# GpSimd makes the low parts of weight units 11, 13, ... 25 in a two-block transformer kernel

## What is computed

```python
mod = silu(c) @ w_ada + b_ada                  # six vectors of 1024: sh1, sc1, g1, sh2, sc2, g2
h = rmsnorm(x, norm_gains[0]) * (1 + sc1) + sh1
proj = h @ w_in                                # queries, keys, values of 16 heads of 64
out_a = attention, heads 0 to 7 (full causal, bias by distance)
out_b = attention, heads 8 to 15 (window of 128, grouped keys, a sink per head)
y = concatenate([out_a, out_b]) @ w_out
x = x + g1 * rmsnorm(y, norm_gains[1])
```

## Time and profile before

| | |
|---|---|
| median of 3 runs | 789.35 us (789.23 to 792.32) |
| the profiled execution's own time | 793.4 us |
| its span in the profile | 791.7 us |
| its mean granted TensorE clock | 0.976 of full speed |

### The profile page before, as it was taken

How to read it: one execution, slowest core, us unless ns; L and a number is a source line. 1 busy time by engine, 2 the same in 40 slices (tenths; PEclk the granted TensorE clock), 3 DMA queues, 4 the chain that set the end, 5 groups by cost and what they waited for, 6 DMA issues and landing times.

```text
span 791.7 us, 12079 instructions
## 1 busy us (share of the span) xinstructions
PE 739.5 (93%) x4062; PEld 622.0 (79%) x4062; DVE 518.5 (65%) x764; ACT 449.5 (57%) x724; POOL 44.3 (6%) x77
## 2 busy tenths in 40 slices
PE   0599999979999999997999999999897999999998
PEld 0498966679999887775989777777686888888886
DVE  6886697678777744348657465665656777677443
ACT  1644677566666443355555587654546777777331
POOL 3100100100000100014102000000000000000000
PEclk9899999969999999999999999999997999999999
DMA  8999985237877655443774554544444566666651
GB/s 319 362 352 319 261 275 161 80 112 218 246 221 250 225 190 184 159 126 102 225 190 130 185 168 135 167 119 135 157 131 132 168 190 176 203 174 201 201 198 55
DMA packets 137166, 150.50 MB, mean 190 GB/s; under 512 B 6163, under 2 KB 111782, under 8 KB 137128
## 3 DMA queue, kind: packets, MB, share of 16 engines
q1 hardware_dynamic: 135278, 145.28, 59.2%
q10 hardware_dynamic: 1852, 4.75, 1.7%
HBM read 148.57 MB, written 1.44 MB: 189 GB/s over the span
## 4 chain that ended last, share of the span: by engine, by line
PE 85%; DVE 6%; ACT 3%; DMA 3%; issue 2%; POOL 0%; SPq 0%; POOLq 0%; DVEq 0%; ACTq 0%
PE acc L1363 14%; PE acc L1365 13%; PE acc L1364 13%; PE acc L1355 11%; PE acc L1342 7%; PE acc L1343 7%; PE acc L1344 7%; PE acc L1356 5%; DMA raw<-in_w_ada 3%; PE aux L1331 2%; PE aux L1527 1%; DVE wl L960 1%; PE aux L1501 1%; PE aux L1496 1%; DVE ada_sum L1038 1%
## 5 line engine op out<-in xcount | busy, mean ns | idle before, releaser
L960 DVE TENSOR_TENSOR wl<-raw,wh 128x1024 fp32r<-128x1024 f32 x217 | 266.0, 1231 | 151.6 <-ACT wh L594 150.8
L594 ACT ACTIVATE wh<-raw 128x1024 fp32r<-128x1024 f32 x217 | 227.9, 1055 | 124.2 <-PE acc L1365 111.3
L1342 PE MATMUL acc<-xT,wh 128*128 128x256 f32 x440 | 127.0, 289 | 5.5 <-DVE xT L990 4.1
L1355 PE MATMUL acc<-xT,wh 128*128 128x512 f32 x352 | 127.1, 405 | 0.8 <-DVE xT L982 0.8
L1343 PE MATMUL acc<-xT,wh 128*128 128x256 f32 x440 | 126.2, 287 | 0.0
L1344 PE MATMUL acc<-xT,wl 128*128 128x256 f32 x440 | 126.2, 287 | 0.0
L1363 PE MATMUL acc<-wh,xT 128*128 128x512 f32 (+1 forms) x272 | 110.0, 404 | 4.7 <-DVE xT L982 2.4
L1365 PE MATMUL acc<-wh,xT 128*128 128x512 f32 (+1 forms) x272 | 105.5, 388 | 0.0
L1364 PE MATMUL acc<-wl,xT 128*128 128x512 f32 (+1 forms) x272 | 105.2, 387 | 0.0
L1356 PE MATMUL acc<-xT,wl 128*128 128x256 f32 x352 | 100.1, 284 | 0.0
L1342 PEld LDWEIGHTS acc<-xT,wh 128*128 128x128 f32 x440 | 86.3, 196 | 7.5 <-issue 5.9
(11 more groups left out here) (260 smaller groups left out, 889.8 us busy)
## 6 DMA issues: line engine op xcount, KB each, us to landing
raw<-in_w_in SPq DMA_DIRECT2D x66, 512.0 KB, 3.6
raw<-in_w SPq DMA_DIRECT2D x64, 512.0 KB, 3.8
raw<-in_w_ffn_in SPq DMA_DIRECT2D x44, 512.0 KB, 4.4
raw<-in_w_ada SPq DMA_DIRECT2D x27, 512.0 KB, 6.2
raw<-in_w_ffn_out SPq DMA_DIRECT2D x22, 512.0 KB, 3.3
raw_more<-in_w_ada SPq DMA_DIRECT2D x13, 512.0 KB, 6.7
raw<-in_w_out SPq DMA_DIRECT2D x13, 512.0 KB, 4.3
rows_tmp<-in_w_ada ACTq DMA_DIRECT2D x8, 512.0 KB
```

The lines of the kernel that those rows point to most:

```text
L594: A(wh[:, s, :], raw_unit, ACT.Copy).then_inc(rounded, 1)
L960: V.tensor_tensor(wl[:, s, :], raw_slot(r), wh[:, s, :].bitcast(f32), ALU.subtract).then_inc(split_ready, 1)
L1342: mm(bank[:, 0:ROWS], wh[:, s, w], hi, start=(kt == 0), stop=False)
L1355: mm(bank[:, :], wh[:, s, w], moving[:, kt, :], start=(kt == 0), stop=False, skip_group_check=True)
```

## The change

For eight units, 11, 13, ... 25, the subtraction is taken from DVE and given to POOL. POOL makes six of them (11 to 21) ahead of its gain product and two (23, 25) behind it, each as soon as ACT has rounded the unit. A new semaphore `low_by_pool` counts them; PE waits for it where it needs such a unit. `split_ready` is still raised by DVE alone: at the next even unit DVE waits for POOL's part and then adds 2.

```diff
+POOL_LOW = [11, 13, 15, 17, 19, 21, 23, 25]
...
+            def low_unit(u):
+
+                pool.wait_ge(rounded, u + 1)
+                s = slot_of(u)
+                nc.gpsimd.tensor_tensor(wl[:, s, :], raw_slot(raw_place(u)[0]), wh[:, s, :].bitcast(f32), ALU.subtract)\
+                    .then_inc(low_by_pool, 1)
+
+            for u in POOL_LOW[:6]:
+                low_unit(u)
             pool.wait_ge(ada_used, (C_G1 + 1) * KT)
             pool.wait_ge(gain_loaded, 16)
             sums = ada_sum[:, D * C_G1:D * (C_G1 + 1)]
             nc.gpsimd.tensor_tensor(sums, sums, G1[:, :], ALU.mult).then_inc(gain_scaled, 1)
+            for u in POOL_LOW[6:]:
+                low_unit(u)
...
-            def low_unit(wait, r, s):
+            def low_unit(wait, r, s, made=1):
 
                 dve.wait_ge(rounded, wait)
-                V.tensor_tensor(wl[:, s, :], raw_slot(r), wh[:, s, :].bitcast(f32), ALU.subtract).then_inc(split_ready, 1)
+                V.tensor_tensor(wl[:, s, :], raw_slot(r), wh[:, s, :].bitcast(f32), ALU.subtract).then_inc(split_ready, made)
 
             def low_static(u):
-                if u < U_END:
-                    low_unit(u + 1, raw_place(u)[0], slot_of(u))
+                if u < U_END and u not in POOL_LOW:
+                    made = 1
+                    if u - 1 in POOL_LOW:
+                        dve.wait_ge(low_by_pool, POOL_LOW.index(u - 1) + 1)
+                        made = 2
+                    low_unit(u + 1, raw_place(u)[0], slot_of(u), made)
...
+            def low_ready(u):
+
+                if u in POOL_LOW:
+                    pe.wait_ge(low_by_pool, POOL_LOW.index(u) + 1)
+                else:
+                    pe.wait_ge(split_ready, u + 1)
```

More of the change, by code:

```diff
@@ L307, in build_program @@
         aux = [ctx.enter_context(nc.psum_tensor(f"aux{i}", [P, 512], f32)) for i in range(4)]
+        low_by_pool = sem("low_by_pool")
         first_full = [sem(f"first_full{i}") for i in range(FIRST_RING)]
@@ L1331, in transpose @@
                 return mm(out, in_, ident[0:n, 0:n], start=True, stop=True, is_transpose=True)
+            def low_ready(u):
[3 more added lines that the diff above has]
+                    pe.wait_ge(split_ready, u + 1)
             def col_unit(u, wait, bank, moving, waits=None):
                 s = slot_of(u)
-                pe.wait_ge(split_ready, wait)
+                if wait is None:
+                    low_ready(u)
+                else:
+                    pe.wait_ge(split_ready, wait)
                 for kt in range(KT):
@@ L1369, in narrow_half @@
                 s = slot_of(u)
-                pe.wait_ge(split_ready, u + 1)
+                low_ready(u)
                 for j in range(2):
@@ L1466, in proj1_unit @@
                         pe.wait_ge(acc_free, k - 3 if k < 8 else (9, 9, 9, 9, 10)[k - 12])
-                    col_unit(k, k + 1, acc[k % 4], xT, (lambda kt: X_COUNT * X_PROJ1 + 4 * (kt // 2) + 4) if k == 0 else None)
+                    col_unit(k, None, acc[k % 4], xT, (lambda kt: X_COUNT * X_PROJ1 + 4 * (kt // 2) + 4) if k == 0 else None)
                 else:
                     pe.wait_ge(acc_free, 11)
-                    pe.wait_ge(split_ready, k + 1)
+                    low_ready(k)
                     for r in range(RT):
@@ L1611, in _ @@
                         pe.wait_ge(acc_free, F_UP1 + k - 5)
-                    col_unit(u, u + 1, acc[(2, 3, 0, 1)[k - 4]], xT)
+                    col_unit(u, None, acc[(2, 3, 0, 1)[k - 4]], xT)
                 elif k < 12:
```

## The result

| | before | changed |
|---|---|---|
| median | 790.45 us, 10 runs (789.01 to 792.87) | 798.42 us, 10 runs (793.73 to 802.32) |
| ratio, 95% interval | | 1.0097 [1.0081, 1.0114] |
| profiled execution, span | 793.4, 791.7 us | 797.16, 795.4 us |

Slower by 0.97%, about 7.7 us, where +3.8 us was forecast; the interval lies above the 0.5% line, and 798.42 us above the range of 790.3 to 797.2. (1.1 us of that distance is the kernel before: 789.35 us from three runs then, 790.45 from ten now. The change itself was forecast at half its size all the same.) The runs also scatter more, 8.6 us against 3.9.

A forecast was written before the change was run, and what follows sets the result against it. PE was taken to bound the kernel, with DVE almost full behind it. The terms 2.6 - 1.5 + 0.5 + 0.8 - 0.3 + 2.25 - 0.55 gave +3.8 us on 789.35, so 793.2 us, range 790.3 to 797.2.

The forecast's parts named there:

- (a): Loads up to w18: 1.05 MB more ahead of them makes w18 and with it head 2 2.6 us later.
- (b): Ada item a28 behind head 2: POOL's gain product no longer holds it there, -1.5 us.
- (c): Unit 19: DVE is spared 1.1 us, POOL subtracts after a31 and a32 waits 1.6 us; net +0.5 us.
- (d): Unit 20's subtraction alone releases w19's slot, so w21 lands late and head 8's reciprocal follows; +0.8 us.
- Rival 1: PE's clock falls to 1.2 GHz after a stop around 124.5 to 127 us; +5.5 to +7.2 us, chance 0.25 (with lateness piling up).
- (e): Unit 21: DVE is spared 1.1 us, a37 waits 0.8 us for POOL's subtraction; -0.3 us.
- (f): POOL's gain product, now behind a37, goes in before a38 and delays it; +2.25 us.
- (g): PE's `weigh` of head 8 waits for the delayed `split` but had slack to spare; -0.55 us.
- rival 4: The two-element copy ahead of scores of heads 8 to 15 also waits for POOL; +4.0 us, chance 0.45 shared with forecast.
- Rival 2: The collisions at 119 to 125 us fall elsewhere, so (f) is gone; +1.6 us, 790.9 us, chance 0.22.
- rival 3: Not slower: w18 lands less than 1.5 us later and (b) outweighs (a); 788.4 to 789.5 us, chance 0.08.

The follow-up runs named there:

- e11: The kernel before, with POOL's gain product moved behind the last score of head 15; 790.64 us, ratio 0.9989.
- e12: e1 with units 19 and 21 back on DVE and the gain product behind unit 17; 790.61 us, ratio 0.9994.
- e14b: e12 with the gain product moved behind the last score of head 15; 790.02 us, ratio 0.9993.
- e1: The changed kernel, but SP gets an odd unit's raw place back from POOL's own semaphore; 793.04 us, ratio 1.0032.
- e3: The changed kernel with POOL's gain product moved behind unit 23; 796.90 us, ratio 1.0077.
- e8: The changed kernel with the edits of e1 and e3 together; 791.43 us, ratio 1.0021.
- e6: The changed kernel with four extra PE products, results unused, in each of the steps of heads 4 and 5; 797.83 us, ratio 1.0087.
- e2: The changed kernel with DVE making all low parts, odd units' raw places still released one unit late; 794.55 us, ratio 1.0057.
- e9: e2 with only units 11, 13 and 15 released one unit late; 794.97 us, ratio 1.0041.
- e13b: The changed kernel with units 19 and 21 back on DVE and released on time, gain product moved ahead to unit 17; 794.79 us, ratio 1.0051.
- e10: e2 with only units 17 to 25 released one unit late, 11 to 15 by their own subtraction; 793.25 us, ratio 1.0023.
- e4: The kernel before, with POOL's gain product waiting until all 40 ada items are used; 791.67 us, ratio 1.0006.

## Why the prediction was wrong

The direction and most of the mechanisms held, and the chance given to slower (0.47) was nearly that given to "within 0.5%"; the size was half of what came.

**What bounds the kernel**: right. PE's 0.9 us of waits were all that could be won (the stages of e11, e12 and e14b are 0.7 us shorter), and DVE at 19.17 of 20 us had no reserve: e1, with two subtractions and the gain product between 100 and 121 us, loses 0.32%, and e12, with none of them there, nothing.

**(a), (b)**: right. 2.6 and 1.28 us were measured, and the stage was 1.1 us late at head 2. w16's rounding came at 80.2 in the stage's time (80.4 said), with 0.7 us of PE's waiting. That this is "taken back before 101 us" is only half so: PE waits 0.54 us at 102.93 for w18's sake, which hides it. In e3's profile w18 came 0.9 us earlier, PE doesn't wait there, and head 2 is still 0.6 us late after 1.3 at head 1.

**(c), +0.5: the step that failed.** It said that POOL begins unit 19 when a31 ends, and so meets a32. But POOL waits for nothing except the rounding, and unit 19 is rounded before a31's turn comes, so POOL goes in first and a31 itself is held. The rows of the kernel before say so already, and the prediction didn't use them: unit 19 was rounded from 100.79 to 101.84, and a31 followed at 102.11.

```profile
100.79 1.05 ACT L594 ACTIVATE wh<-raw 128x1024 fp32r<-128x1024 f32 x1
```

```profile
102.11 1.28 DVE L1038 SCALAR_TENSOR_TENSOR ada_sum<-raw,cT,ada_sum 128x1024 f32<-128x1024 f32 x1
```

A subtraction of 2.39 us from 101.9 on ends at 104.3, and a31 1.08 us behind it, at 105.4 instead of 103.39: an estimate of 2.0 us of hold from the rows of before, where 2.2 was measured. It counts in full, because a31 stands ahead of head 4's reciprocal, and the subtraction that DVE was spared (1.1 us) behind it. All kernels with unit 19 on POOL bear this out. In us from the start of each span; the last column is the time from head 2's `weigh` to head 3's, less the 3.61 of before:

| kernel | unit 19 rounded | a31 recorded | POOL starts | held up | step at head 3 |
|---|---|---|---|---|---|
| changed | 103.96 | 103.99 | 104.03 | a31, 2.2 us | 2.2 us |
| e3 | 103.39 | 103.76 | 103.46 | a31, 1.9 us | 1.8 us |
| e1 | 100.37 | 101.33 | 100.45 | a31, 1.3 us | 1.25 us |
| e8 | 100.40 | 101.40 | 100.47 | a31, 1.2 us | 1.2 us |
| e6 | 104.51 | 104.40 | 104.59 | POOL, then a32, 1.0 us | 0.9 us |

Only in e6, where ACT had waited 0.26 us for w19, was unit 19 late enough for a31 to be first. That w19 is issued 10 us later in the stage's time (99.38, and 88.44 before) was not followed by the sum either, but it worked towards the assumed order, not against it.

**Rival 1, 0.25, happened**: PE's clock. I had put it at the stop of 124.5 us; it followed the 2.1 us stop of step (c), and cost 1.6 us more in this profile. (The 3.4 us stretch that rival 1 reckons with stands in none of its rows; the trace of before has one at 358 to 362 us.) It differs from profile to profile: those of e2 and e9 have 6.8 us of it, those of e3 and e13b, with stops of 1.7 and 1.8 us, none. That it makes the scatter of 8.6 us is likely and not shown: the mean granted clock of each execution was 0.972 in the slowest of the changed kernel (802.32 us), 0.980 in the fastest (793.73) and 0.976 to 0.979 between, and in e3 0.970 at 801.34 and 0.981 at 791.80. But this is a mean over the whole program, and e6 has 0.972 at 798.88 us, 1.9 us above its fastest.

**(d), +0.8: right in place, too small for the release alone.** w21 was issued at 114.92 (113 said, and 112.43 in e10, where nothing else is late), and landed some 5.3 us later where 4.3 was taken from the earlier trace rows. Without the late w18 (e10) it costs 1.5 us of the stage and 0.23% of the time. In the changed kernel most of it was hidden by lateness that was there already, the slow clock's among it: ACT waited only 0.61 us for w21.

**(e), (f), (g) with rival 4**: +2.25 - 0.3 - 0.55 forecast, and together with (d) +2.2; the stage lost 1.6 there. The copy of two elements did wait (rival 4, without which the gain product would have met a38 and not a37), and PE did wait for `split` at head 8. Rival 4's price, "within the forecast", was right.

**Sum of the profile**: 1.1 + 2.2 + 1.6 + 1.6 = 6.5 us, where the prediction had 1.1 + 0.5 + 0 + 2.2; the other 1.2 us of the 7.7 in the medians aren't in this profile, and stay open. By the experiments, late release alone costs 0.57%, exclusion with the release mended 0.32%, together 0.89 of the 0.97%, each to about 0.2 (e2) or 0.13 (e1).

**Rival 2** (the collisions miss) and **rival 3** (not slower) didn't happen; e8 shows what rival 2 would have looked like with the release mended.

**The rule on the two engines.** The Trainium skill (SBUF — State Buffer, "Who interferes with whom") says that DVE's two-input instructions, and copies in its two-port modes, contend with POOL, and that whoever issues first holds the shared ports for the whole instruction. The runs agree on all partners: subtraction, ada item, and a copy of two elements that waits 2.1 us. "First" can't be read off DVE's recorded starts: a31 is recorded 0.04 us ahead of POOL's instruction and still waited for it. The end of the DVE instruction ahead of it, 104.08 there, puts it behind.

## What to carry to other kernels

Moving work from DVE to an idle POOL relieves nothing where DVE is full, because DVE stands still for up to twice what it was spared: subtractions on POOL at 63 to 86 us cost nothing that could be measured (e12), and about 0.3% went with two more and the gain product between 100 and 121 (e1). Who goes first at a meeting can often be read from the trace of before: compare when the input of the moved instruction is ready with when the other engine's next one starts. Before moving it, follow every semaphore that the moved instruction raised: the late return of a buffer, which no engine's busy time shows, was probably the larger part here (0.57% alone in e2, 0.65 less when e1 takes it away, against 0.32 that stays; the intervals of e1 and e2 overlap). And when PE bounds a stage, a stop of 2 us may cost nearly twice its length through the clock (2.1 + 1.6 here), so price a change by its longest stop too, and not only by the sum of them.

## What the runs showed of the hardware that was not expected

A copy of 128 x 2 float32 on DVE, SBUF to SBUF, that takes 0.16 us stood 2.34 us behind a POOL product (e4). In the rows shown here, a POOL instruction that waited for an ada item (1.0 us in e6, 0.9 in the changed kernel) went in right behind it, and the next ada item or two-element copy on DVE waited until it had ended. POOL's subtraction of 128 x 1024 float32 takes 2.35 to 2.40 us unhindered, the same as its product. Stops of PE of 1.7 to 1.8 us were followed by 6.8 us at 1.2 GHz in e2 and e9 and by none in e3 and e13b: the length of the stop alone doesn't decide, and what does was not found.
